# Head 0's value weights carry the forget gate's columns, its values are made early, and no load waits for another: a two-layer GLA and pooling step on 8 Trainium2 cores

## The reference

```python
z = xn @ w_in
q, k, v, ga, u, gb, alow, mg = jnp.split(z, IN_OFFSETS, axis=-1)      # alow: 16 columns
la = jax.nn.log_sigmoid(alow @ w_alpha + b_alpha) / GATE_TAU          # forget gate, 512 wide
o, S = gla_scan(q, k, v, la, S0, chunk)       # 4 heads, key width 128, value width 256, causal
o = rms_per_head(o) * gla_gain * silu(ga)
y_pool = pool_mix(u, ...)                     # trailing means over 2/4/8/16 tokens, 4 groups
merged = sigmoid(mg_a) * (o @ w_a) + sigmoid(mg_b) * ((y_pool * silu(gb)) @ w_b)
h = h + merged @ w_out
```

## Time and profile before

| | |
|---|---|
| median of 3 runs | 1225.57 us (1224.73 to 1225.89) |
| profiled execution | 1224.85 us, span of its slowest core 1223.1 us |
| spans of the 8 cores | 1221.9 to 1223.1 us |
| mean granted PE clock | 0.986 to 0.989 |
| busy: PE, DVE, ACT, POOL | 1151.9, 676.9, 573.5, 467.0 us |
| DMA | 118.90 MB, mean 97 GB/s |

### The profile page before, as it was taken

The page is one execution under the profiler, slowest core; times in us unless marked ns, Lnnn a source line. Parts: engine busy times, 40 slices in busy tenths (PEclk is TensorE's granted clock), DMA queues, the critical chain, the costliest instruction groups (busy, mean ns, idle before and its releaser), DMA issues.

```text
span 1223.1 us, 22742 instructions; the slowest of 8 cores (1221.9 to 1223.1 us)
## 1 busy us (share of the span) xinstructions
PE 1151.9 (94%) x7616; PEld 691.5 (57%) x7616; DVE 676.9 (55%) x1255; ACT 573.5 (47%) x1279; POOL 467.0 (38%) x754
## 2 busy tenths in 40 slices
PE   1579899999999999999999999999999999999997
PEld 1245457767676555555545555676777555555543
DVE  4466877766765222226776776666667422223555
...
GB/s 200 90 155 40 19 76 159 101 136 76 105 87 175 31 39 58 18 30 157 139 158 140 105 47 87 144 71 121 86 89 93 186 33 59 35 19 26 178 166 155
DMA packets 68591, 118.90 MB, mean 97 GB/s; under 512 B 4188, under 2 KB 46556, under 8 KB 68442
## 3 DMA queue, kind: packets, MB, share of 16 engines
...
## 4 chain that ended last, share of the span: by engine, by line
PE 85%; DVE 4%; ACT 3%; issue 3%; POOL 2%; DMA 1%; SPq 0%; DVEq 0%; POOLq 0%; ACTq 0%
PE bank L551 83%; PE bank L556 3%; DMA sb_OT<-wal 1%; POOL sb_OT L579 1%; ACT sb_Y L570 1%; DVE sb_X L598 1%; DVE sb_X L591 1%; ACT L570 1%; ACT sb_OT L570 1%; DVE sb_Y L585 0%; DVE sb_ast L579 0%; DVE sb_XN L579 0%; DVE sb_MB L811 0%; DVE sb_Y L591 0%; POOL sb_rst L579 0%
## 5 line engine op out<-in xcount | busy, mean ns | idle before, releaser
L551 PE MATMUL bank<-sb_XN,sb_RG 128*128 128x384 bf16 (+2 forms) x3280 | 664.4, 346 | 10.8 <-DVE sb_XN L579 4.4
L551 PEld LDWEIGHTS bank<-sb_XN,sb_RG 128*128 128x128 bf16 x3280 | 316.3, 98 | 248.1 <-issue 8.2
L591 DVE SCALAR_TENSOR_TENSOR sb_X<-sb_X,bank 128x384 f32<-128x384 f32 (+2 forms) x240 | 140.7, 594 | 255.1 <-PE bank L551 234.0
L570 ACT ACTIVATE sb_X<-bank,sb_halfc 128x384 f32<-128x384 f32 (+2 forms) x160 | 97.9, 615 | 250.0 <-PE bank L551 214.4
L570 ACT ACTIVATE sb_X<-bank 128x256 bf16<-128x256 f32 (+6 forms) x328 | 145.9, 464 | 96.2 <-PE bank L551 80.7
L579 POOL TENSOR_TENSOR sb_MB<-sb_X 128x384 bf16<-128x384 f32 (+2 forms) x80 | 88.0, 1100 | 203.7 <-DVE sb_X L591 203.3
L551 PE MATMUL bank<-sb_OT,sb_RG 128*128 128x384 bf16 (+2 forms) x680 | 143.6, 344 | 5.5 <-DVE sb_OT L591 4.2
L551 PE MATMUL bank<-sb_RG,sb_XN 128*128 128x256 bf16 (+1 forms) x1088 | 145.5, 272 | 1.1 <-ACT sb_OT L570 1.1
L570 ACT ACTIVATE sb_Y<-sb_Y 128x1024 bf16<-128x1024 f32 (+1 forms) x79 | 83.5, 1057 | 120.9 <-DVE sb_Y L591 101.6
L551 PE MATMUL bank<-sb_RG,sb_MB 128*128 128x512 bf16 (+1 forms) x544 | 125.3, 379 | 0.0
L579 POOL TENSOR_TENSOR sb_OT<-sb_OT 128x398 f32<-128x398 f32 (+12 forms) x122 | 112.5, 922 | 30.1 <-ACT sb_OT L570 14.0
...
## 6 DMA issues: line engine op xcount, KB each, us to landing
sb_RG<-wpk POOLq DMA_DIRECT2D x40, 512.0 KB, 8.3
sb_Y<-sgla SPq DMA_DIRECT2D x32, 512.0 KB, 4.3
nsg_s<-sb_Y SPq DMA_DIRECT2D x32, 512.0 KB, 2.8
sb_Y<-xp SPq DMA_DIRECT2D x28, 512.0 KB, 5.1
sb_RG<-wpk POOLq DMA_DIRECT2D x16, 896.0 KB, 10.8
H<-sb_Y SPq DMA_DIRECT2D x16, 512.0 KB, 3.6
sb_Y<-H SPq DMA_DIRECT2D x16, 512.0 KB, 3.8
y_p<-sb_Y SPq DMA_DIRECT2D x16, 512.0 KB, 2.6
```

The lines of the kernel that those rows point to most:

```text
L551: return S.add("pe", lambda e: e.matmul(out, lhsT=lhsT, rhs=rhs, start=start, stop=stop, skip_group_check=sgc), r=r, w=w, cost=c, lat=300. ...
L570: return S.add("act", lambda e: e.activation(out=out, in_=in_, func=func, **kw), r=r, w=w, cost=c, lat=150.0, tset=tset)
L591: return S.add("dve", lambda e: e.scalar_tensor_tensor(out=out, in0=in0, scalar=scalar, in1=in1, op0=op0, op1=op1), r=r, w=w, cost=ecost(" ...
```

## The change

The 16 gate columns stand beside the 256 value columns of head 0 (`VA` = 272), so a matmul with a token tile as stationary operand gives both, with the tokens on the partitions. `va_unit` replaces `alpha`: for each tile eight matmuls of 272 columns, one ACT copy of the values, four small DVE operations that split the 16 gate columns in three parts and lay them out in eight blocks (`ast_tok`), one PE transpose; from there on the gate goes as before. The values of head 0 are kept in the first quarter of `OT`'s chunk (`v_of`), which the output of head 0 overwrites at the end of its `att_unit`; so `va_unit` runs where `alpha` ran, and `att_unit` of head 0 makes no values. `load_al` and its broadcast copy are gone. All waits of loads on landings (`after`, `xafter`) are gone. The ring has 35 cells, some loads have other cells, and in layer 1 the fourth pooling weight and head 0's other blocks are recorded later. The scheduler gives the two queues a bus each, at 130 bytes/ns until `weave` of chunk 4, and then 230 (SP) and 280 (POOL).

```diff
-RING = 36
+RING = 35
-        dma_free = [0.0]
+        dma_free = {"sp": 0.0, "pool": 0.0}
...
-                done_t[idx] = xfer_start + op["cost"] + 1800.0
+                done_t[idx] = xfer_start + op["cost"] + (1800.0 if e == "sp" else 4500.0)
...
+        q_rate = {"sp": 130.0, "pool": 130.0}
...
-                    xdma[t] = dma(h_ap[:, :], xp[(t - 1) * 128:t * 128, :], r=[], w=hk,
-                                  after=xafter.get(t, ()) if l < 0 else ())
+                    xdma[t] = dma(h_ap[:, :], xp[(t - 1) * 128:t * 128, :], r=[], w=hk)
...
+        def v_of(h, c, p):
+
+            if h > 0:
+                return v_tok[p][0], lambda j, m=1: v_tok[p][1][2 * j:2 * (j + m)]
+            o = 8 * C_OFF[c] + (2 * NM if c == 0 else 0)
+            return OT[:, o:o + 2 * (C_LEN[c] - (NM if c == 0 else 0))], lambda j, m=1: ["ot%d_0" % c]
...
+        def va_unit(l, c, wv):
             N = C_LEN[c]
-            ba, bak = bank("P")
-            proj(ba[:, 0:N], wal[0], wal[1], c, bak)
-            cp("act", ast[:, 0:N], ba[:, 0:N], r=[bak], w=["ast"])
-            tt("dve", ar1[96:128, 0:N], ba[96:128, 0:N], ast[96:128, 0:N], ALU.subtract, r=[bak, "ast"], w=["ar1"])
-            tt("dve", ast[32:64, 0:N], ba[32:64, 0:N], ast[32:64, 0:N], ALU.subtract, r=[bak, "ast"], w=["ast"])
-            cp("act", ast[96:128, 0:N], ar1[96:128, 0:N], r=["ar1", "ast"], w=["ast"])
-            tt("dve", ast[96:128, 0:N], ar1[96:128, 0:N], ast[96:128, 0:N], ALU.subtract, r=["ar1", "ast"], w=["ast"])
+            v_ap, v_k = v_of(0, c, 0)
+            for j, t in enumerate(CHT[c]):
+                n = t_len(t)
+                bv, bvk = bank("P")
+                for kc in range(8):
+                    mm(bv[0:n, 0:VA], xn_tile(t, kc), wv[0][:, kc * VA:(kc + 1) * VA], kc == 0, kc == 7,
+                       r=wv[1] + ["xn%d" % t], w=[bvk])
+                jj = j - (1 if c == 0 else 0)
+                if t == 0:
+                    cp("act", v0[0:n, :], bv[0:n, 0:256], r=[bvk], w=v0_k)
+                else:
+                    cp("act", v_ap[:, jj * 256:(jj + 1) * 256], bv[0:n, 0:256], r=[bvk], w=v_k(jj))
+                a4 = ast_tok[0:n, 128 * j:128 * j + 128].rearrange("p (b m) -> p b m", m=16)
+                al_ = bv[0:n, 256:VA].unsqueeze(1)
+                r4 = alr[0:n, 16 * j:16 * j + 16].unsqueeze(1)
+                ak = ["att%d" % j]
+                cp("dve", a4[:, 0:4, :], al_.to_broadcast([n, 4, 16]), r=[bvk], w=ak)
+                tt("dve", r4, al_, a4[:, 0:1, :], ALU.subtract, r=[bvk] + ak, w=["alr%d" % j])
+                cp("dve", a4[:, 4:6, :], r4.to_broadcast([n, 2, 16]), r=["alr%d" % j], w=ak)
+                tt("dve", a4[:, 6:8, :], r4.to_broadcast([n, 2, 16]), a4[:, 4:6, :], ALU.subtract,
+                   r=["alr%d" % j] + ak, w=ak)
+                yield
+            bt, btk = bank("G")
+            btb = bfv(bt)
+            o = 0
+            for j, t in enumerate(CHT[c]):
+                n = t_len(t)
+                tr(btb[:, o:o + n], ast_tok[0:n, 128 * j:128 * j + 128], ident_bf[0:n, 0:n],
+                   r=["att%d" % j, "ident_bf"], w=[btk])
+                o += n
+            cp("act", ast[:, 0:N], btb[:, 0:N], r=[btk], w=["ast"])
...
-            for j in range(0, nt, 2):
+            for j in range(0, nt, 2) if h > 0 else ():
...
             if l == 0:
-                wal = load_al(0)
+                wh = [None] * 3
+                wh[1] = load_h(0, 0, 1)
                 wb = [load_b(0, 0)]
                 consts()
-                for t in CHT[0][0:3]:
+                va0 = va_unit(0, 0, wh[1])
+                for t in CHT[0]:
                     run(stage_d(-1, t, None))
+                    next(va0)
                 build_wst(0, "dve")
-                run(stage_d(-1, 3, None))
                 pool_pre(0)
-                wb.append(load_b(0, 1, after=[xdma[2]]))
-                wpw = wload(0, WP_PW, 512, 4, after=[xdma[2]])
-                xafter.update({4: [wdma[1]], 5: [wdma[1]], 6: [wdma[1]], 7: [wdma[2]], 8: [wdma[2]], 9: [wdma[2]]})
-                weave(al_(0) + b_((0, 0), (0, 1)), d_tiles(-1, 1, None))
-                wb.append(load_b(0, 2, after=[xdma[6]]))
-                weave(al_(1) + b_((1, 0), (1, 1), (0, 2), (1, 2)), d_tiles(-1, 2, None))
+                wb.append(load_b(0, 1))
+                wpw = wload(0, WP_PW, 512, 4)
+                wh[0] = load_h(0, 0, 0)
+                weave([(va0, 3.0)] + b_((0, 0), (0, 1)), d_tiles(-1, 1, None))
+                wb.append(load_b(0, 2))
+                wh[2] = load_h(0, 0, 2)
+                wb.append(load_b(0, 3))
+                weave(va_(1) + b_((1, 0), (1, 1), (0, 2), (1, 2)), d_tiles(-1, 2, None))
...
+                q_rate.update(sp=230.0, pool=280.0)
...
                 for c in range(1, NCH):
-                    weave(m_units(l - 1, c, wl), d_tiles(l - 1, c - 1, wo), al_(c - 2) if c > 1 else [])
+                    weave(m_units(l - 1, c, wl), d_tiles(l - 1, c - 1, wo), va_(c - 2) if c > 1 else [])
...
-                weave(d_tiles(l - 1, 4, wo) + al_(3) + al_(4), b_(*c4))
-                wh = load_h(l, 0)
-                weave(b_((2, 0), (2, 1), (2, 2), (2, 3)), a_(0))
+                weave(d_tiles(l - 1, 4, wo) + va_(3), b_(*[(c, g) for c in (0, 1) for g in range(3)]))
+                wb.append(load_b(l, 3))
+                wh[0] = load_h(l, 0, 0)
+                wh[2] = load_h(l, 0, 2)
+                weave(b_((2, 0), (2, 1), (2, 2), (0, 3), (1, 3), (2, 3)), va_(4) + a_(0))
```

More of the change, by code:

```diff
@@ L362, in make_consts @@
         cf[a, CF_ROWMASK + (a // TS if a < NS else NSS)] = 1.0
-    for blk, m in ((0, 0), (1, 1), (2, 0), (3, 1), (4, 2), (6, 0)):
+    for blk, m in ((0, 0), (1, 1), (2, 2), (4, 0), (5, 1), (6, 0)):
         cf[16 * blk:16 * blk + 16, CF_SPLIT + m] = 1.0
@@ L456, in build_nc @@
             kT.append(X.take(512, BF16))
-            v_tok.append(X.take(1024, BF16))
         kdT, kdT_k = X.take(512, BF16)
@@ L464, in build_nc @@
         S_bf = [X.take(256, BF16) for _ in range(2)]
+        v_tok = [X.take(1024, BF16) for _ in range(2)]
         S_in = [Y.take(1024) for _ in range(2)]
@@ L507, in ot_rest @@
             return ["ot%d_%d" % (c, h) for h in range(1, 4)] + (["ots_%d" % h for h in range(1, 4)] if c == 0 else [])
-        mrg = []
-        for i in range(2):
-            a = X.take(512, at=2048 + i * 4096)
-            b = X.take(512, at=2048 + i * 4096 + 2048)
-            mrg.append((a, b))
-        a = X.take(512, at=0)
-        b = X.take(512, at=10240)
-        mrg.append((a, b))
+        mrg = [(X.take(512, at=o0), X.take(512, at=o1)) for o0, o1 in ((2048, 4096), (21504, 6144), (0, 13312))]
         Y.pos = 0
@@ L803, in alpha @@
                 act(b_ap(c, h), bl[:, 0:N], AF.Exp, r=[blk, "negc"], w=b_keys(c, h),
[L804 removed]
+                    bias=negc[:, 4 * l + h:4 * l + h + 1], scale=-1.0)
             yield
@@ L960, in att_unit @@
             yield
-            if c == 0:
+            if c == 0 and h > 0:
                 bv, bvk = bank("P")
@@ L1182, in load_c, with load_h @@
             return wload(l, WP_C + cb * 3584, 3584, WC_AT[cb])
-        def load_h(l, h, after=()):
-            o = WP_H + h * 6144
-            return [wload(l, o + 2048 * i, 2048, WH_AT[h][i], after=after) for i in range(3)]
+        def load_h(l, h, part=None):
+            o = WP_H + h * 6144 + (128 if h else 0)
+            if part is not None:
+                w_ = 8 * VA if h == 0 and part == 1 else 2048
+                return wload(l, o + 2048 * part + (128 if h == 0 and part == 2 else 0), w_, WH_AT[h][part])
+            return [load_h(l, h, i) for i in range(3)]
         def d_tiles(l, c, wo):
@@ L1200, in a_, with va_ @@
                 return [(att_unit(l, 0, c, *wh), 11.0)]
-            def al_(c):
-                return [(alpha(l, c, wal), 2.5)]
+            def va_(c):
+                return [(va_unit(l, c, wh[1]), 7.0)]
             def s_(*js):
@@ L1272, in build_nc @@
         wl = [load_c(l, cb) for cb in range(LAST, 8)]
-        wo = [wload(l, WP_O + i * 2048, 2048, 17 + 4 * i) for i in range(4)]
+        wo = [wload(l, WP_O + i * 2048, 2048, 14 + 4 * i) for i in range(4)]
         dma(fgf, fg_d[:, :], r=[], w=fgf_k)
@@ L1301, in _pack_weights @@
         W = w_in[l]
-        wp[l, :, WP_AL:WP_AL + 128] = W[:, C_AL:C_AL + 16].reshape(8, 128, 16).transpose(1, 0, 2).reshape(128, 128)
         for g in range(4):
```

81 lines of the change are left out of this document (38 added, 43 removed).

## The result

The changed kernel takes 1242.7 us (median of 5 runs), the kernel before 1225.89 on the same chip: a ratio of 1.0134 with an interval of 1.0113 to 1.0156, slower by 17 us where 19.5 us less were forecast. From here on a time with a number in brackets is the median of that many runs in which every core had a mean granted clock of 0.975 or more; the others show cores with a lower clock and a longer time, whatever the kernel. "Per core" is the median span of all cores at that clock. The changed kernel so takes 1242.2 us [4], from 1235.43 to 1248.31, and 1231.5 us per core. The profiled run took 1248.31 us. Its cores, all alike before, now differ: spans of 1224.1 (core 2) to 1246.8 us (core 7), and which core is late changes from run to run.

What follows compares the result with a forecast made beforehand. The front was taken as bound by ACT's order and the wait for x, the layer border by PE. Gains of 1 + 8 + 2 + 5.5 (front) and 3 (layer 1), 19.5 us, gave 1206 us; range 1195 to 1219.

Steps and rivals of the forecast that it cites:

- The loads: All loads: unwaited loads share the engines with x, and moved loads come long before they are needed; taken as 0.
- 83 to 175 us: Layer 0 after the front: PE loses 10.8 us of alpha and value work, half becomes time: 5.5 us, ends 2 and 11.
- Chunks 1 and 2: Layer 0's front: ACT squares and scales tiles earlier, chunk 2 complete at 72 us, PE's stall gone: 8 us, ends 3 and 11.
- Given back: Rival: POOL and DVE set the pace from 83 us, layer 1 gives 1 us; 9 us gained, 1217; chance 0.18.
- PE work: Both layers: PE does 5.5 us less in each; layer 1 gives 3 us, layer 0's share counted in the front's stretches.
- The clock: Layer 0's front: without the stall the second slow piece at the lower clock goes: 2 us, ends 0 and 2.
- x is crowded out: Rival, front: weight queue keeps half the engines until 45 us, tile 6 is 4 us late; 14.5 us gained, 1211; chance 0.10.
- POOL is held: Rival, start: POOL stands behind its queued loads, tile 0's scale is 21 us late; 1232, slower; chance 0.06.
- DVE and ACT: Each layer: 12 us of small DVE operations come, 9 us go; ACT's value copies cost what dropped gate copies cost; nothing added.

Runs made afterwards that it cites:

- e3: The changed kernel with the old transfer model in its planner (one shared path at 230 bytes per ns, 1.8 us landing): 1226.7 us.
- e14: The changed kernel with its planner on one shared path at 230 bytes per ns, keeping the 4.5 us landing on POOL's queue: 1223.6 us.
- e13: The changed kernel with its planner landing POOL's transfers after 1.8 us instead of 4.5, two separate paths kept: 1242.6 us.
- e9: The changed kernel with the old transfer model, a third state buffer (not for layer 1's first head) and the loads' waits put back: 1219.8 us.
- e7: The kernel before with head 0's values made by one matmul per tile instead of eight, in both layers: 1216.7 us.
- e8: The changed kernel with the old transfer model and the loads' waits put back, two weight blocks of head 0 recorded later: 1224.6 us.
- e4: The kernel before with every explicit wait of a load for another load taken off: 1231.7 us.

## Why the prediction was wrong

**The step that failed first** is *The loads*, in its last sentence: "The other moves (ring cells, merge buffers, value buffers) fall in stretches where PE is busy 25 of 25 us; a load that comes late there would cost, but each has a whole merge or head before it is needed: 0." It looked at weight loads. The lines of the diff that give each queue a path of its own got no term at all, though they place every instruction, and the loads that came late were sample states, which have two buffers and one store ahead of each load. The rule on shared DMA engines was weighed there for x alone. Going back to the old model gives 15.5 us (e3), and e14 and e13 show that the two paths are what costs in it. This explains the loss against the kernel before; all of the forecast gain is still missing then.

**The step that failed second** is *83 to 175 us* ("I let half become time: 5.5 us") together with the 8 us of *Chunks 1 and 2*. The mechanism of the latter was right: chunk 2's tiles are squared 15 us earlier, the stall before 80.70 us is gone, and 12 us of idle are filled by 83.1 us. But head 0's scores come at 116.1 to 121.5 us in the versions with early values (the changed kernel, e3, e9), hardly earlier than before (118.3 to 121.4), and PE waits later instead. With the state waits cured, layer 0 gives 270.7 - 262.6 = 8.1 us up to head 2's scores (e9), not 16.5, and 3.4 us without the third buffer and the load waits (e3). That is what the rival *Given back* said would happen, though its price of 9 us in all was not reached: the best version gains 4.5. e7 shows the reason for the part in head 0's stage: it returns 4.6 us of the 13 to 16 us of PE work taken from it. Why the earlier chunk 2 brings no earlier scores is not shown by a run of its own.

**PE work.** In layer 1 the size of the step came out in e9 alone: 3 forecast, and 699.49 - 271.38 + 92.2 = 520.3 us of border and head 0 become 433.6 + 83.9 = 517.5, of which 0.8 are lost again behind head 1's first scores. In the changed kernel the same two stretches take 434.1 + 94.5 us. PE's busy time did not fall by 12 us: the median of the eight cores goes from 1152.5 to 1151.0 (e9: 1145.8), and on the slowest core it rose by 3.3. One part is in the front: before 58 us the 48 early value matmuls of whole tiles took 10.0 us on core 7, 0.21 us each, where the 128 of layer 1's border took 17.3 us, 0.135 each.

**The clock.** Two stretches below 1.00 remain in the first 200 us on core 7, 29.9 to 57.7 us (0.82) and 109.8 to 200 us (0.88, 0.96 and 0.93); the second has moved, not gone: it stands where PE now idles (5.6 of 30.2 us in the first of its rows). The 2 us did not come.

**x is crowded out** was put at 5 us; the crowding is there: tile 6 lands at 36.7 us on core 7, before at 32.7 (core 1), the 4 us of that rival. But ACT squares it at 46.82 us and waits for no such load, as *The loads* said. Its cost is 2.4 us at most in the changed order of work (e8), and 7 us in the order of the kernel before (e4). **POOL is held** was wrong: POOL issued two rows of four loads in 2.95 and 2.84 us and came to tile 0's scale at 10.80 us; the ninth load did wait for a landing, 3.0 us, as the prediction said. **DVE and ACT** at 0: DVE's busy time rose by 5.5 us, and PE waited 1.7 us for one `sb_alr` piece in layer 1; no experiment priced this alone.
